# Two transformer blocks on one core: the second block's context stream moved ahead of the first block, its expert rows gathered beside it

## What is computed

```python
x = first_block(x, c, ctx, ...)       # mLSTM, differential attention, SSD, merge, conv FFN
xl, xc = x, ctx_2                     # second_block, layer 0 and 1
yc, yl = deltanet_mixer(hc, hl, ...)  # layer 0: the latent scan starts from the context's
                                      # final states s_f, s_b
xl = xl + g1l * yl;  xl = xl + g2l * peer(mod(norm(xl)), ...)
xc = xc + g1c * yc;  xc = xc + g2c * peer(mod(norm(xc)), ...)
_, yl = attention_mixer(hc, hl, ...)  # layer 1: keys and values from xc and xl
xl = xl + g1l * yl;  xl = xl + g2l * peer(...)   # latent tokens only
return rmsnorm(xl, final_g)

def peer(h, ...):   # per token: 8 heads x 16 chosen of 16384 experts = 128 rows
    idx, gate = topk(...)             # two top-16 over 128 keys, then top-16 over 256 pairs
    act = gelu(einsum('pd,phkd->phk', h, u_tab[idx]))
    return einsum('phk,phkd->pd', gate * act, v_tab[idx])
```

## Time and profile before

| | us |
|---|---|
| median of 3 runs | 5280.2 (5278.64 to 5284.21) |
| the profiled execution | 5276.41 |
| its span in the trace | 5274.7 |

### The profile page before, as it was taken

The page is one execution under the profiler, slowest core; times in us unless marked ns, Lnnn a source line. Parts: engine busy times, 40 slices in busy tenths (PEclk is TensorE's granted clock), DMA queues, the critical chain, the costliest instruction groups (busy, mean ns, idle before and its releaser), DMA issues.

```text
span 5274.7 us, 45722 instructions
## 1 busy us (share of the span) xinstructions
PE 4244.9 (80%) x15314; PEld 2302.6 (44%) x15314; DVE 2888.3 (55%) x5960; ACT 846.3 (16%) x1852; POOL 1227.2 (23%) x1173
## 2 busy tenths in 40 slices
PE   7988789899978888887888777777687766677877
PEld 3333334754468787774574222222222224522222
DVE  3343321424546666663135887877876633688665
ACT  2231220006411111111011001001010022100001
POOL 0000000001034443340001333343343300133433
PEclk9988899999989898898999999999999988899999
DMA  4433242440010000002113989999999941398998
GB/s 178 152 112 128 112 161 95 184 152 34 32 40 1 1 1 1 1 1 80 64 57 153 398 342 407 388 354 399 352 387 422 421 166 40 123 397 332 420 421 357
DMA packets 128923, 1037.05 MB, mean 197 GB/s; under 512 B 14256, under 2 KB 14640, under 8 KB 16304
## 3 DMA queue, kind: packets, MB, share of 16 engines
q0 software_dynamic: 110592, 805.36, 38.1%
q1 hardware_dynamic: 18096, 228.77, 11.6%
HBM read 1030.93 MB, written 3.15 MB: 196 GB/s over the span
## 4 chain that ended last, share of the span: by engine, by line
PE 46%; DVE 29%; issue 8%; DMA 7%; POOL 5%; ACT 5%; DVEq 0%; POOLq 0%; SPq 0%; ACTq 0%
PE bank L192 27%; DVE arena L2484 9%; DMA arena<-in_uv,arena 6%; PE bank L1887 4%; POOL arena L2463 4%; ACT arena L204 4%; DVE arena L2489 3%; PE bank L2441 3%; DVE arena L210 3%; PE bank L1898 2%; PE bank L1500 1%; DVE arena L214 1%; ACT L204 1%; POOL arena L1980 1%; PE bank L1908 1%
## 5 line engine op out<-in xcount | busy, mean ns | idle before, releaser
L2441 PE MATMUL bank<-arena 128*128 128x512 f32 x3072 | 1550.8, 631 | 494.8 <-DVE arena L2489 494.5
L192 PE MATMUL bank<-arena 128*128 128x512 f32 (+4 forms) x5408 | 1625.9, 459 | 112.8 <-ACT arena L204 48.7
L192 PEld LDWEIGHTS bank<-arena 128*128 128x128 f32 (+1 forms) x5408 | 861.1, 182 | 828.1 <-issue 670.0
L2441 PEld LDWEIGHTS bank<-arena 128*128 128x128 f32 x3072 | 535.6, 193 | 1506.7 <-DVE arena L2489 1078.5
L2463 POOL DMA_INDIRECT arena<-in_uv,arena x768 | 808.4, 1053 | 1466.6 <-PE bank L2441 884.5
L2484 DVE CUSTOM_DVE_ANT_0 arena<-arena 128x1024 f32<-128x1024 f32 x768 | 942.4, 1227 | 278.4 <-DMA arena<-in_uv,arena 212.4
L204 ACT ACTIVATE arena<-arena 128x1 f32<-128x1 f32 (+7 forms) x1070 | 309.5, 289 | 2863.0 <-DVE arena L2484 1852.8
L204 ACT ACTIVATE arena<-bank 128x512 f32<-128x512 f32 (+4 forms) x512 | 283.4, 554 | 1393.6 <-PE bank L192 646.5
L2489 DVE TENSOR_SCALAR arena<-arena 128x128 f32<-128x128 f32 x768 | 292.5, 381 | 285.1 <-ACT arena L204 267.0
L1980 POOL TENSOR_TENSOR arena<-arena 128x512 f32<-128x512 f32 x224 | 285.7, 1276 | 448.6 <-PE bank L1887 356.3
L1887 PE MATMUL bank<-arena 128*128 128x128 f32 x1792 | 281.0, 313 | 65.2 <-POOL arena L1980 65.2
(11 more groups left out here) (238 smaller groups left out, 2504.8 us busy)
## 6 DMA issues: line engine op xcount, KB each, us to landing
arena<-in_ada_w SPq DMA_DIRECT2D x24, 2048.0 KB, 8.1
arena<-in_w_in SPq DMA_DIRECT2D x16, 2048.0 KB, 8.0
arena<-in_w_mod SPq DMA_DIRECT2D x12, 2048.0 KB, 8.2
arena<-in_dn_w SPq DMA_DIRECT2D x12, 2048.0 KB, 8.2
arena<-in_w_up SPq DMA_DIRECT2D x11, 2048.0 KB, 8.1
arena<-in_wq SPq DMA_DIRECT2D x8, 2048.0 KB, 8.1
arena<-in_uv,arena POOLq DMA_INDIRECT x768, 9.8
arena<-in_w_down SPq DMA_DIRECT2D x5, 2048.0 KB, 7.2
```

The lines of the kernel that those rows point to most:

```text
L192: t = p.e.matmul(out, l, r, start=(i == 0), stop=(i == n - 1))
L2441: t = p.e.matmul(by[half], m["dg"][ee % 4], m["uv"][r][:, 1024 + 512 * half:1536 + 512 * half], start=(ee == 0), stop=(ee == 127))
```

## The change

The context tiles of the second block's layer 0 need nothing of the first block. The delta-net now runs twice, on two tiles each: first for the context (`delta(0)`), whose final states go to DRAM (`S_out`), and after the first block for the latent tiles (`delta(1)`), which reads them back. After `delta(0)` the context's norm and queries follow (`cquery`), then the first block. Beside that block DVE chooses the context's experts (`dve_cselect`), and Pool gathers their rows from two separate tables, U rows (4 KB) and V rows (4 KB): 512 indirect DMAs into six buffers, in the order of `order`. DVE forms the 256 dots; the 256 V rows are scaled and added by DVE (`scalar_tensor_tensor`), every third of them by Pool (two instructions). PE has no part in it. `cend` adds the sum to the context tiles. `peer` of layer 0 then has two tiles in place of four.

How the added DVE work is spread: `beside` makes one or more steps of it before each explicit wait of a stage, in proportion to their count (172 choosing steps over `mo`; 32, 120 and 80 gather steps over `sp`, `do` and `mr`), and `PACE` puts four steps into each tick of `sout` and behind each of the 44 channels of the FFN. The first block's ring has two slots in place of four. The 12 MODS chunks of `ada_w0` come first, and four more before `n1`; the other 20 lie beside `mhead` and `sout`. Scores, buffers and indices lie in the other two ring slots.

```diff
-    MODS = ([(0, "w_mod", c, 0, "b_mod") for c in range(12)] + [(1, "ada_w0", c, 2, "ada_b0") for c in range(12)]
+    MODS = ([(1, "ada_w0", c, 2, "ada_b0") for c in range(12)] + [(0, "w_mod", c, 0, "b_mod") for c in range(12)]
...
     def chunks(self, e, m, prep, inverse, recur, zfirst):
-        for k in range(17):
-            paced(([((inverse or none)(e, m, k), 1)] if k < 16 else []) + ([((recur or none)(e, m, k - 1), 4)] if k else [])
+        for k in range(9):
+            paced(([((inverse or none)(e, m, k), 1)] if k < 8 else []) + ([((recur or none)(e, m, k - 1), 4)] if k else [])
...
+        r["order"] = ([("u", 0, e) for e in range(128)] + [(w, n, e) for e in range(128) for w, n in (("v", 0), ("u", 1))]
+                      + [("v", 1, e) for e in range(128)])
...
+    def pools(self, e):
+        return e % 3 == 1
+    def dve_back(self, v, m):
+        for q, (w, n, e) in enumerate(m["order"]):
+            slot, c = m["slots"][q % 6], m["acts"][n][:, e:e + 1]
+            if w == "u":
+                v.wait_ge(m["sem"][q % 6], 16 * (q // 6 + 1))
+                v().tensor_tensor_reduce(slot, slot, m["ht"][n], 1.0, 0.0, ALU.mult, ALU.add, c).then_inc(*V.up("cb.dot", n, e))
+            elif not self.pools(e):
...
+                v.wait_ge(m["sem"][q % 6], 16 * (q // 6 + 1))
+                y = m["y"][n][0]
+                t = v().scalar_tensor_tensor(y, slot, c, y, ALU.mult, ALU.add) if e else ts(v, y, slot, c, None, ALU.mult, None)
+                t.then_inc(*V.up("cb.v", n, e))
+            yield
+    def pool_back(self, g, m):
+        def add(q):
+            w, n, e = order[q]
+            if w == "v" and self.pools(e):
...
+                    g().tensor_scalar(slot, slot, c, None, ALU.mult).then_inc(*G.up("cb.cv"))
+                    g().tensor_tensor(y, y, slot, ALU.add).then_inc(*G.up("cb.v", n, e))
+        for q, (w, n, e) in enumerate(order):
+            if q > 3:
+                add(q - 4)
...
+                w_, n_, e_ = order[q - 6]
+                if w_ == "u":
+                    g.wait_ge(*V.of("cb.dot", n_, e_))
+                else:
+                    g.wait_ge(*(G if self.pools(e_) else V).of("cb.v", n_, e_))
+            g.e.indirect_dma_start(out=m["slots"][q % 6], out_offset=None, in_=self.I["u0" if w == "u" else "v0"],
...
+    def beside(self, e, gen, num, stage):
+        total, n = self.sizes.get((e.steps.name, stage), 1 << 30), [0, 0]
+        def step():
+            n[0] += 1
+            while n[1] * total < n[0] * num and n[1] < num:
+                n[1] += 1
+                next(gen, None)
...
+    def dve_program(self, v):
+        run(self.dve_mod(v, 0, 12))
+        self.dve_norm(v, "cn", L["cn"], xt, [0, 1], "n1_0", M[1], 0, 1, hP)
+        self.after(v, "cn")
+        self.dve_delta(v, 0)
...
+        rest = self.beside(v, sel, 172, "mo")
...
+        rest = self.beside(v, back, self.PACE["sp"], "sp")
...
+    PACE = dict(sp=32, so=4, do=120, mr=80, ff=4)
```

More of the change, by code:

```diff
@@ L100, in __call__ @@
         if self.steps.last:
-            self.wait_ge(*self.steps.last)
+            self.wait(*self.steps.last)
         return self.e
@@ L1517, in dve_ffn @@
                                   ).then_inc(*V.up("ff.act", j // 2))
+            for _ in range(self.PACE["ff"]):
+                next(back, None)
         v.wait_ge(*A.of("ff.row", 1))
@@ L1702, in pe_ngates @@
             yield
[L1703 to L1706 removed]
+            p.wait_ge(*V.of(f"ng{m['i']}.gx", d))
+            p.wait_ge(*A.of(f"ng{m['i']}.be", d))
+            b = self.banks.take(p, f"ng{m['i']}.tr", d)
+            for i in range(2):
                 o = 16 * i
@@ L2495, in dve_peer @@
             v.wait_ge(*P.of(k + ".y", n, 127))
-            for s in range(2):
-                if s == 1 or t0 == 0:
-                    v.wait_ge(*A.of(f"{k}{s}.row", 1))
+            for s in m["sides"]:
+                v.wait_ge(*A.of(f"{k}{s}.row", 1))
             for half in range(2):
@@ new lines, in pools, with dve_cselect @@
+    def pools(self, e):
+        return e % 3 == 1
+    def dve_cselect(self, v, m):
+        V, ij = self.V, m["ij"]
+        for n in range(2):
+            m["s16"], m["c1"] = heads(m["sc"][n], 16), m["sc"][n]
+            yield from self.dve_choose(v, m, "cb", n, "cq.s")
+            v().scalar_tensor_tensor(ij[:, 0], ij[:, 0], 128.0, ij[:, 1], ALU.mult, ALU.add).then_inc(*V.up("cb.i"))
+            v().tensor_copy(heads(m["idx"][n], 8), ij[:, 0]).then_inc(*V.up("cb.idx", n))
+            yield
+            g3 = heads(m["gates"][n], 8)
+            v().tensor_tensor(g3, m["best"], bc(m["best"][:, :, 0], 2, 16), ALU.subtract).then_inc(*V.up("cb.g", n))
+            yield
@@ new lines, in dve_coefs @@
+    def dve_coefs(self, v, m, n):
+        V, A, smx, g3 = self.V, self.A, m["smx"], heads(m["gates"][n], 8)
+        v.wait_ge(*A.of("cb.g", n))
+        red(v, smx[:, 0:8], g3, ALU.add).then_inc(*V.up("cb.gs"))
+        v().reciprocal(smx[:, 8:16], smx[:, 0:8]).then_inc(*V.up("cb.gs"))
+        v().tensor_tensor(g3, g3, bc(smx[:, 8:16], 2, 16), ALU.mult).then_inc(*V.up("cb.gate"))
+        v.wait_ge(*A.of("cb.act", n))
+        v().tensor_tensor(m["acts"][n], m["acts"][n], m["gates"][n], ALU.mult).then_inc(*V.up("cb.coef", n))
@@ new lines, in pe_cend, with act_cend, dve_cend @@
+    def pe_cend(self, p, m):
+        self.pe_bcast(p, "ce", m["wide"])
+    def act_cend(self, a, m):
+        self.act_bcast(a, "ce", m["g2"])
+    def dve_cend(self, v, m):
+        V, A, G, D = self.V, self.A, self.G, self.D
+        v.wait_ge(*G.of("cb.v", 1, 127))
+        self.dve_bcast(v, "ce", self.M[1][:, 40:48, 1], m["wide"])
+        v.wait_ge(*A.of("ce.row", 1))
+        v.wait_ge(*D.of("xc.in", 0))
+        for n in range(2):
+            y0, y1 = m["y"][n]
+            v().tensor_tensor(y0, y0, y1, ALU.add).then_inc(*V.up("ce.y"))
+            v().tensor_tensor(y0, y0, m["g2"], ALU.mult).then_inc(*V.up("ce.y"))
+            v().tensor_tensor(self.x[:, n, :], self.x[:, n, :], y0, ALU.add).then_inc(*V.up("ce.x"))
@@ L2934, in dve_program @@
         self.dve_mout(v, m, self.yT)
+        rest()
         self.after(v, "mo")
+        rest = self.beside(v, back, self.PACE["sp"], "sp")
         self.dve_sproj(v, L["s"])
-        self.dve_sout(v, L["s"], self.yT, self.every(2, some))
+        rest()
+        self.dve_sout(v, L["s"], self.yT, self.every(2, some, back))
+        run(mods)
         self.after(v, "so")
+        rest = self.beside(v, back, self.PACE["do"], "do")
         self.dve_dproj(v, L["d"])
-        weave_lag([self.dve_dhead(v, L["d"], n) for n in range(8)], some)
+        weave_lag([self.dve_dhead(v, L["d"], n) for n in range(8)])
@@ L3000, in act_program @@
         self.after(a, "mo")
+        for n in range(2):
+            a.wait_ge(*self.V.of("cb.g", n))
+            act(a, L["cq"]["gates"][n], L["cq"]["gates"][n], ACT.Exp).then_inc(*A.up("cb.g", n))
         self.act_sproj(a, L["s"])
         self.act_sout(a, L["s"], self.every(2, some))
+        run(mods)
+        self.act_back(a, L["cq"], 0)
         self.after(a, "so")
         self.act_dproj(a, L["d"])
-        weave_lag([self.act_dhead(a, L["d"], n) for n in range(8)], some)
+        weave_lag([self.act_dhead(a, L["d"], n) for n in range(8)])
@@ L3056, in pool_program @@
         self.pool_setup(g)
+        self.after(g, "cn")
+        self.pool_delta(g, 0)
+        self.after(g, "q0n")
+        self.after(g, "cq")
+        if self.stop < 1:
+            return
         m = L["m"]
+        g().iota(L["cq"]["iota"], pattern=[[1, 16]], base=0, channel_multiplier=0, allow_small_or_imprecise_dtypes=True
+                 ).then_inc(*G.up("cb.iota", 0))
+        back = self.pool_back(g, L["cq"])
         weave_lag([self.pool_mhead(g, m, n) for n in range(8)])
         self.after(g, "mo")
-        self.pool_sout(g, L["s"])
+        for _ in range(self.PACE["sp"] + 4):
+            next(back)
@@ L3094, in build @@
                     (self.G, self.pool_program), (self.D, self.sp_program))
-        for steps, program in programs:
-            program(Engine(Count(), steps))
+        self.sizes = {}
+        for _ in range(2):
+            for steps, program in programs:
+                steps.reset()
+                steps.table = {}
+                program(Engine(Count(), steps))
+            self.banks.reset()
+            for r in self.rings:
+                r.reset()
         for S, _ in programs:
```

1307 lines of the change are left out of this document (735 added, 572 removed).

## The result

The changed kernel takes **5624.5 us** (median of 3 runs, 5621.48 to 5625.38) against 5280.2: a ratio of 1.0649 (95% interval 1.0625 to 1.0673). The profiled execution took 5624.49 us, with a span of 5622.8. The forecast was 5507 us, 4.3% slower, with a range of 5260 to 5680; measured are 6.5%.

What follows compares the result with a forecast made beforehand. It took PE to bound the first block before, and Pool, gathering and adding rows, to bound the added work there. Outside 3771 us plus first block 1730 make 5501 us of span, so 5507 us, 4.3% slower (range 5260 to 5680).

Steps and rivals of the forecast that it cites:

- Outside the first block: All stages before and after the first block: 3771 us in place of 4163, a gain of 392 us.
- chunks: Delta-net run two tiles at a time: nine passes in place of 17, 508 us a side.
- Inside: The first block with the added work beside it: seven stage terms sum to +618 us, giving 1730 us.
- the merge: First block's merge, 163 us: four items before the last gate, 70 following at 2.2 us; +84 us (70 to 109).
- the price of an item on Pool: Pool's gathers at 1.24 us, own V rows at 4.7: 2.0 us an item alternating, 2.8 in the last 128.
- stage 4: `dproj` and `dhead`, base 199 us: 120 items at 2.2 us are 264, so +65 us (41 to 100).
- Rival E: First block: DVE's in-order waits cost nothing, PE stays the bound; block grows 55 us, kernel 4940 us; chance 0.02.
- The hold-up of gathers: Added DVE work with two SBUF inputs and Pool's delay each other: 2.2 and 2.9 us an item taken.
- rival B: Stages 4 to 6: no lock on the gathers, 2.0 and 2.8 us an item; kernel 5446 us; chance 0.14.
- Rival C: Stages 4 to 6: Pool's adds are cheap, 1.9 us a V row gives 5226 us, faster; chance 0.13.
- Rival D: First block: two-slot loads and gathers contend, choosing hidden nowhere; about 5740 us; chance 0.13.
- the signs it named: FFN channels every 8 to 12 us, Pool over 85% busy to n3, add about 2.5 us, `peer` 787.

Runs made afterwards that it cites:

- bare: Run 1's kernel with nothing beside the first block: no choosing, gathers, dots or rows, the context's peer output left out; 4764.9 us (one run).
- run 8: The changed kernel with Pool's scaling left out and its addition of two SBUF tiles kept; 5438.1 us (one run).
- run 2: On top of run 1, each dot and V row on DVE cut to 8 of 1024 columns, all gathers and waits kept; 5177.1 us (one run).
- run 1: The changed kernel with all 256 V rows added by DVE and none by Pool, which only gathers; 5355.7 us (1.0152 to the kernel before).
- run 7: The changed kernel with Pool's addition left out and its scaling kept; 5427.7 us (one run).
- run 3: The changed kernel with Pool scaling and adding only 512 of the 1024 columns of its V rows; 5465.3 us (one run).
- run 10: On top of run 2, each gather brings 2 KB a token in place of 4, with as many instructions and waits; 5057.1 us (one run).

## Why the prediction was right in sign and short in size

**Outside the first block** it had 3771 us, the trace 3716. The opening (119, measured 116), `dnproj` (184; 182, ACT busy for 129 of it, as said), the queries (75; 67), MODS with n1 (62; 64) and `peer` (787; 795) come out near. `chunks` was taken too long: 508, measured 482 and 490, which makes 44 of the 55 us.

**Inside** it had +618 us, the trace shows +795. With the columns of the table: the order alone gives -60 (bare), the choosing +64 (mLSTM, 247 to 311), the gathers at half their bytes +228, the other half +121, DVE's dots and rows in full +174, and 86 of the rows moved to Pool +269. That sums to 796; taken off in another order the shares could differ.

Stage by stage: mLSTM +79 (forecast +55, in its bounds), `sproj` +2 (+23), `sout` +94 (+72), FFN +350 (+304, in its bounds), tail and `ff.y` +17 (+15); `dproj` with `dhead` +133 where it had 65 (41 to 100), and the merge +119 where it had 84 (70 to 109), both outside.

**The step that failed most** is the price of an item on Pool: "a product of two 128 x 512 tiles takes 1.276 us, a one-input form 0.634. I double both". The addition was right (2.5; median 2.35, mean 2.59). The scaling by a column took 2.89 us where it had 1.27: the masking in the earlier trace rows is no stand-in for it. With the waits a row came to 6.0 us where it had 4.7. 84 times 1.62 us are 136 us of Pool's time, not all of it on the path: leaving the whole scaling out took 243 us off Pool and saved 186 (run 8), so by that proportion the excess was worth about 104 us (an estimate), most of the 117 by which the whole was short.

The Trainium skill (GPSIMD Engine Reference, Elementwise — side-by-side cycle accounting) has 769 ns for 512 elements, from which an estimate for this scaling is 1.54 us; by the trace that is little more than half the price.

**That the size came out within some 2% is partly luck.** Two more terms were wrong, and their errors go opposite ways. First, the base of stage 4: the prediction left `dproj` and `dhead` at 199 us, although it had itself moved twelve MODS chunks to the opening. The bare stage is 152, so what the work added there is 180 us, not 133. Second, it took Pool as the only bound besides the stages' own time. Gathers alone, by that, give some 5000 us (run 2's theory A); run 2 took 5177. There the DMA, at 0.97 in the FFN, and the time that DVE stands for a landing came on top. In the changed kernel's own FFN the DMA was busy for 0.60, and the bandwidth is not what held it. The sentence "that its rows are 4 and not 8 KB changes the bytes, not the number of rows" is true of Pool's price and looks past that bound. The stated range was wide as well: its lower end, 5260 us, lay under the kernel before.

Three small slips in the working moved nothing in the forecast. DVE's 349 of 1112 us leave out n2's 6. Pool's lower bound of 1.9 us a row holds no waits, though the 4.7 do. Rival E's Pool sum has 4.3 us a row where 4.7 was taken.

**The hold-up of gathers** was bounded by 0.4 us an item and taken at 0.2 (2.2 for 2.0 us) and 0.1 (2.9 for 2.8). The mean gather is 0.94 us without long DVE work (run 2), 1.28 with all of it (run 1), 1.20 in the changed kernel: 0.3, somewhat more than it took. So rival B is refuted.

The Trainium skill (SBUF — State Buffer, Who interferes with whom) infers that DVE's second SBUF input leaves descriptor writing alone; for this kernel's dots and V rows the gathers of runs 1 and 2 contradict it. The other direction, Pool's addition holding up DVE, was named and not priced: DVE's V rows took 1.71 us for 1.28. The same page of the Trainium skill has such a DVE instruction contend with any GpSimd one that reads SBUF, and makes no difference between forms; runs 7 and 8 show one (1.34 us beside the scaling, 1.52 beside the addition).

**Rival C** had the right lever: with no rows on Pool the kernel is 269 us faster. It was still 1.5% slower than before. Rows that stay on Pool and are cheap were not tried below run 3's price; the changed kernel and run 3 give 69 us for each us of the two instructions, and by that even 1.26 us (C's 1.9 less 0.64 of waits) would leave the kernel at some 5335 us (an estimate): cheap adds alone would hardly have turned the sign. **Rival D**'s contention shows in runs 2 and 10, between gathers and weights for bandwidth; for the two slots no run shows it. **Rival E** stays far: bare and choosing together would be about 4830 us (4764.9 + 64).

Of the signs it named: the FFN's channels came every 11.8 us (8 to 12 was said), Pool's addition at a mean of 2.59 us (2.5), `peer` at 795 and 790 (787). ACT was busy for 78 of the 94 us from the start of `dnproj`. Pool over 85% busy held in the FFN alone (87%); it was 37% in `sproj`, 55% in `sout`, 79% in `dproj` and `dhead` and 59% in the merge, where DVE and PE stood for 79 us in turn.

## What to carry to other kernels

Work put beside another stage was cheap here where the engine that carries it would otherwise wait for one long stretch of another's: 80 items with the merge, 50 of them ahead of its gate wait, cost 18 us and 52 ahead of `ff.y` some 21, while items between short steps that PE waits for cost up to 2 us each (83 us for the step from 132 to 176 in the FFN), rising with the load. Before a price is doubled from a like instruction, ask whether it is the same form; a row of the wrong form cost Pool 136 us here, and the kernel about 104 by run 8's proportion. And when a stage moves, take its old share out of the base that it left.
